# The experts' row parts laid out anew: high parts in first halves, low parts in second halves, buffers by parity

## The reference

```python
def _swiglu(h, wg, wu, wd):
    return (jax.nn.silu(h @ wg) * (h @ wu)) @ wd

def _moe(h, router, wg, wu, wd):
    ...
    y = jnp.zeros_like(xt)
    for e in range(N_EXPERTS):
        y = y + gates[:, e:e + 1] * _swiglu(xt, wg[e], wu[e], wd[e])
    return y.reshape(shp)
```

## Time and profile before

| | us |
|---|---|
| median of 3 runs (lowest, highest) | 1505.51 (1504.45, 1506.86) |
| the profiled execution | 1503.68 |
| its span | 1501.9 |
| TensorE matmuls busy | 1459.6 (97%) |
| VectorE busy | 1095.7 (73%) |
| ScalarE busy | 877.5 (58%) |

### The profile page before, as it was taken

One profiled execution on the slowest core, in us unless ns is written; L12 is line 12 of the kernel. 1 busy time (PEld: TensorE's weight loads), 2 busy tenths in 40 slices (PEclk: granted clock), 3 DMA queues, 4 the chain that ended last, 5 costly groups with the idle time before them and its releaser, 6 DMA issues.

```text
span 1501.9 us, 26668 instructions
## 1 busy us (share of the span) xinstructions
PE 1459.6 (97%) x11549; PEld 1203.7 (80%) x11549; DVE 1095.7 (73%) x1029; ACT 877.5 (58%) x868; POOL 147.7 (10%) x179
## 2 busy tenths in 40 slices
PE   6999999999999988999999999999999999999997
PEld 6999999999979977877767777777777777777774
DVE  5687455554378964223698898888988888888897
ACT  4445443433366623342577777777777777777775
POOL 0056100000200041232300000000000000000110
PEclk9999999999999999999899999999999999999999
DMA  7653564545335120144799999999999999999991
GB/s 232 198 156 96 157 226 162 165 126 156 102 106 177 57 59 5 35 139 164 263 355 402 387 369 380 382 377 392 365 376 386 374 390 365 367 388 371 393 405 62
DMA packets 250317, 378.05 MB, mean 252 GB/s; under 512 B 28217, under 2 KB 142121, under 8 KB 249906
## 3 DMA queue, kind: packets, MB, share of 16 engines
q1 hardware_dynamic: 247922, 370.04, 69.2%
q0 software_dynamic: 2064, 6.18, 1.2%
q10 hardware_dynamic: 208, 0.07, 0.0%
HBM read 368.47 MB, written 7.78 MB: 251 GB/s over the span
## 4 chain that ended last, share of the span: by engine, by line
PE 94%; DVE 3%; issue 1%; ACT 1%; DMA 0%; ACTq 0%; DVEq 0%
PE bank L2656 48%; PE bank L2020 29%; PE bank L2333 1%; PE bank L2315 1%; PE bank L2563 1%; PE bank L2588 1%; PE bank L2665 1%; PE bank L2073 1%; PE bank L2503 1%; PE bank L2143 1%; PE bank L2511 1%; DMA vecrows<-b_w 0%; PE bank L2193 0%; DVE wL L1700 0%; PE bank L2647 0%
## 5 line engine op out<-in xcount | busy, mean ns | idle before, releaser
L1700 DVE TENSOR_TENSOR wL<-ering,wH 128x2048 fp32r<-128x2048 f32 x263 | 602.7, 2296 | 82.1 <-ACT wH L1166 80.7
L1166 ACT ACTIVATE wH<-ering 128x2048 fp32r<-128x2048 f32 x264 | 505.9, 1917 | 141.9 <-PE bank L2656 141.7
L2656 PE MATMUL bank<-wH,xgH 128*96 128x512 f32 (+1 forms) x768 | 290.0, 378 | 0.5 <-DVE wL L1700 0.5
L2656 PE MATMUL bank<-wL,xgH 128*96 128x512 f32 (+1 forms) x768 | 287.2, 374 | 0.0
L2656 PE MATMUL bank<-wH,xgL 128*96 128x512 f32 (+1 forms) x768 | 287.1, 374 | 0.0
L2656 PEld LDWEIGHTS bank<-wH,xgL 128*96 128x96 f32 x768 | 124.5, 162 | 44.0
L2656 PEld LDWEIGHTS bank<-wH,xgH 128*96 128x96 f32 x768 | 124.5, 162 | 43.5 <-issue 1.5
L2656 PEld LDWEIGHTS bank<-wL,xgH 128*96 128x96 f32 x768 | 124.6, 162 | 41.6
L2656 PE MATMUL bank<-wH,hH 128*96 128x512 f32 x352 | 139.7, 397 | 0.3 <-DVE wL L1700 0.3
L2656 PE MATMUL bank<-wH,hL 128*96 128x512 f32 x352 | 138.3, 393 | 0.0
L2656 PE MATMUL bank<-wL,hH 128*96 128x512 f32 x352 | 137.9, 392 | 0.0
(11 more groups left out here) (462 smaller groups left out, 2599.2 us busy)
## 6 DMA issues: line engine op xcount, KB each, us to landing
ering<-m_w_gate SPq DMA_DIRECT2D x88, 1024.0 KB, 7.2
ering<-m_w_up SPq DMA_DIRECT2D x88, 1024.0 KB, 7.6
ering<-m_w_down SPq DMA_DIRECT2D x88, 1024.0 KB, 7.4
arena<-a_w_in SPq DMA_DIRECT2D x16, 1024.0 KB, 5.4
arena<-b_w_rkv SPq DMA_DIRECT2D x12, 1024.0 KB, 5.1
fring<-f_w_gate SPq DMA_DIRECT2D x11, 1024.0 KB, 5.0
fring<-f_w_up SPq DMA_DIRECT2D x11, 1024.0 KB, 5.0
fring<-f_w_down SPq DMA_DIRECT2D x16, 704.0 KB, 4.4
```

The source lines that it names most:

```text
L1166: s_.activation(wH[:, hslot(g), :], ering[:, eslot(g), :], ACT.Copy).then_inc(S["e_hi"], 1)
L1700: v.tensor_tensor(wL[:, hslot(g), :], ering[:, eslot(g), :], wH[:, hslot(g), :].bitcast(F32), ALU.subtract).then_inc(S["e_lo"], 1)
L2656: mm = t.matmul(dst, lhs[l], rhs[r], start=(start and m == 0), stop=(stop and m == 2), skip_group_check=True)
```

## The change

Two buffers of the same size and in the same place as before, each with 8 places of 2 x 96 elements, are used in another way. For expert e, the high parts go to the first halves of the places in one buffer and the low parts to the second halves of the places in the other. Even experts take `xgA` for the high and `xgB` for the low parts, odd experts the other way round. The lines that write them and the matmul that reads them follow.

```diff
-        xgH, xgL = [sb(name, [P, DC, 2 * CAP], F32R) for name in ("xgH", "xgL")]
+        xgA, xgB = [sb(name, [P, DC, 2, CAP], F32R) for name in ("xgA", "xgB")]
+        xgH = [x[:, :, 0, :] for x in (xgA, xgB)]
+        xgL = [x[:, :, 1, :] for x in (xgB, xgA)]
...
-                    s_.activation(xgH[:, 4 * j:4 * j + 4, CAP * (e % 2):CAP * (e % 2) + CAP],
+                    s_.activation(xgH[e % 2][:, 4 * j:4 * j + 4, :],
...
-                    o = CAP * (e % 2)
-                    v.tensor_tensor(xgL[:, 4 * j:4 * j + 4, o:o + CAP],
+                    pair = (xgH[e % 2], xgL[e % 2])
+                    v.tensor_tensor(pair[1][:, 4 * j:4 * j + 4, :],
                                     banks[2 + j][:, 0:4 * CAP].rearrange("p (c s) -> p c s", c=4),
-                                    xgH[:, 4 * j:4 * j + 4, o:o + CAP].bitcast(F32), ALU.subtract).then_inc(S["e_xgd"], 1)
+                                    pair[0][:, 4 * j:4 * j + 4, :].bitcast(F32), ALU.subtract).then_inc(S["e_xgd"], 1)
...
-                    o = CAP * (e % 2)
+                    pair = (xgH[e % 2], xgL[e % 2])
...
-                            mm = product(banks[b][0:CAP, 0:w], [x[:, kk, o:o + CAP] for x in (xgH, xgL)],
+                            mm = product(banks[b][0:CAP, 0:w], [x[:, kk, :] for x in pair],
```

## The result

The changed kernel takes 1510.62 us (median of 20 runs, 1505.81 to 1516.33), the kernel before 1505.42 (20 runs, 1501.10 to 1514.43). The ratio is 1.0033, with a 95% interval of 1.0024 to 1.0043: slower by 5 us (3.6 to 6.5). The forecast was +2.1 us, with no change as the likeliest class. The time lies in the range, but it is a loss that can be measured where I held no change for likeliest, and more than twice the forecast.

A forecast was written before the change was run, and what follows sets the result against it. TensorE's pace of starting matmuls was taken to bound the experts' stage. The 512-column matmuls' +2.4 us and the 256-column ones' -0.3 us sum to +2.1 us, added to the median 1505.51 us: 1507.6 us, range 1501.3 to 1511.5.

The forecast's parts named there:

- What bounds the kernel: Experts' stage: it runs at TensorE's pace of starting matmuls, busy 97% of the span, with no wait of TensorE.
- The half matters: Gate and up loads: 512-column pace follows the half, 230.0 ns for first halves, 231.7 or about 226.7 for second.
- The pace before: Gate and up matmuls before the change: on average 229.3 ns for 512 columns, 118.0 ns for 256.
- The pace after: 512-column gate and up matmuls after the change: 230.6 ns, the mean over three loads, +2.4 us over 1920 matmuls.
- The slower rival: Gate and up loads: changing halves costs by itself, mean 233.3 ns, +7.4 us, 1512.9 us; chance 15%.
- The 256-column term: 256-column gate and up matmuls: from 118.0 to 117.3 ns, -0.3 us over 384 matmuls.
- The writes: ScalarE's 16 writes of high parts (484 ns each) and VectorE's 16 of low parts (549 ns): no change.
- The first rival: Gate and up: second-half loads keep averaging 228.6 ns, +0.1 us, 1505.6 us; chance 20% together with the next rival.
- the faster one: Gate and up: the mixture locks all loads into the fast pace of 226.7 ns, -5.3 us, 1500.2 us; chance 20%.
- The chances: Whole kernel's time: faster 0.2, same 0.5, slower 0.3, with slower meaning over 3.0 us.

The follow-up runs named there:

- the mirror: Against the changed kernel, high parts moved to second halves and low parts to first halves; 1506.85 us in one execution.

## Why the prediction was right or wrong

**What bounds the kernel** was right: TensorE's pace, no wait. No wait of TensorE came up, and 6.4 of the 7.1 us between the spans are in the gate and up matmuls.

**The half matters** was right, and the experiments turned it from a reading into a result: with one half for all, both parities have one length, 93.8 or 93.5 us, and the swap of buffers alone changes nothing. The rule in the Trainium skill that TensorE's two read ports are independent ("SBUF — State Buffer", section "Who interferes with whom") would have given no change. The runs disagree with it: two kernels with the same instructions differ by 5 us by where the loads start.

**The pace before** (229.3 and 118.0 ns) was right.

**The pace after** is the term that failed, by its size and by the step that made it: that each load costs what its half costs. The sum took (2 x 230.0 + 231.7) / 3 = 230.6 ns for the mixture, from the down pieces, which go at the mean of their two halves. It is 232.2 to 235.6 ns, 233.3 on average. The term of +2.4 us should have been +7.7. The mean held for six loads of one half and then six of the other, and it turned out to hold for second, second, first; it doesn't hold for first, first, second. Nor is it one load's price elsewhere: an odd expert's pace of 231.7 ns in the kernel before is made of distances of 228, 233, 230 and 236 ns in turn, give or take 1, a pattern of four matmuls where the loads repeat every three.

The slower rival, "changing halves costs by itself", gave 233.3 ns and 1512.9 us. Its mean is the measured one, but by luck. It priced every low part at 240 ns and the others at 230. The 240 was a distance of 236 ns that the unmixed pieces of expert 3 have too, and in the slowest stretches of the changed kernel every distance is 235 or 236 ns, with none at 230. Half right it was in that the mixture costs over the mean; but the mirror changes the half just as often and pays nothing over the mean. I gave it 15% because the down pieces spoke against it, but they change halves twice in twelve loads and the change does it eight times in twelve; the down pieces were no close row for that.

**The 256-column term** had the right sign: 117.3 ns forecast, 115.5 to 115.9 measured, -0.9 us in place of -0.3.

**The writes** of the parts at nothing: right, 465 to 491 ns on ScalarE in the changed kernel, as in the earlier trace rows.

**The first rival** (the odd experts' fast share stays) and **the faster one** (all at 226.7) fell with the timeline: from expert 1 on no piece of 512 columns went below 232 ns in the changed kernel. **The chances**: "same" had 50% and "slower" 30%; the result is slower, by 5 us where the prediction counted a change from 3.0 us on. The measured +5 us is less than the +6.4 of the profile; the kernel with both parts in one buffer has the same expert lengths and a ratio of 1.0046, so the true cost is likely at the upper end of the interval, but the runs don't settle that.

## What stays open

The runs don't show what decides between the two paces of second-half loads (231.7 and 226.7 ns), nor between 232.3 and 235.2 in the changed kernel. Most changes come at a gap that the hidden transposes make, where the next start is 0.5 us after the last, and the new pace then lasts. But not all do: in the kernel before, expert 7 falls back to the slow pace at piece 12, and the largest distance between two starts there is 0.25 us. Most experts of one parity repeat the paces within a run, but not all, and neither the buffer nor the relative place alone decides them. Nor is it shown why first, first, second costs more than its mean and the mirror doesn't, nor by what means the place of a load works on the pace at all; that its reading and that of the weights get in each other's way would fit, but no run tests it.

## What to carry to other kernels

Where TensorE is the bound and reloads its stationary operand for each matmul, measure the distance of starts over a stretch of 40 or more, per layout of the operands: layouts that differ by 32 to 128 bytes in where the operands start went at anything from 226.7 to 235.2 ns, 4% apart, and no wait, count or mean duration showed it. Give all stationary operands of such a stream one place relative to the moving operand, and try the few places; the mixture of this change cost more than the worst single place did. The gain of that is small: the best single place took about 1.8 us of 1505 off the kernel before, barely clear of nothing, and the others nothing that could be measured. Don't price a mixture by the mean of its parts unless a row has the same pattern.

## What the runs showed of the hardware that I had not expected

- At the granted clock of 1.00 (2.4 GHz), a 512-column float32r matmul with a 96-column load before it started 226.7, 228.3 to 229, 230.0, 231.2, 231.7, 232.3 or 235.2 ns after the last one, by the layout and by something kept since an earlier gap. These are means of whole pieces. The 256-column one went at 115.4 to 120.0 ns, and in another order: second halves are the slowest there and the mixture the fastest.
- Exact repetition: in the changed kernel as before it experts 2, 4 and 6 have one length to 0.01 us, and three layouts that differ in buffers only have 94.74 and 94.30 us alike.
